# Moving transposed value blocks by GpSimd copies instead of transfers, in a two-layer decoder step on one core

## The reference

```python
for i in range(2):
    h = rms_norm(x, norm_pre[i])
    a, b, c, z = split(h @ w_in[i], 4)
    if i == 0:   o = b * conv3(c * a) * silu(z)
    else:        # a = q, b = forget gate, c = values; per head, f = lb + (1-lb)*sigmoid(b), k = 1-f
        # S_t = diag(f_t) S_{t-1} + k_t^T v_t ;  o_t = silu(q_t) S_t
        o = rms_norm(o_per_head, onorm) * silu(z)
    x = x + rms_norm(o @ w_out[i], norm_post[i])
```

## Time and profile before

| | us |
|---|---|
| median of 3 runs | 1010.6 (1010.59 to 1011.26) |
| the profiled execution, its own time | 1010.66 |
| its span in the trace | 1008.8 |
| TensorE busy | 1001.4 (99% of the span) |
| VectorE busy | 752.8 (75%) |
| ScalarE busy | 429.9 (43%) |
| GpSimd busy | 18.3 (2%) |

### The profile page before, as it was taken

How to read it: one execution, slowest core, us unless ns; L and a number is a source line. 1 busy time by engine, 2 the same in 40 slices (tenths; PEclk the granted TensorE clock), 3 DMA queues, 4 the chain that set the end, 5 groups by cost and what they waited for, 6 DMA issues and landing times.

```text
span 1008.8 us, 20437 instructions
## 1 busy us (share of the span) xinstructions
PE 1001.4 (99%) x7755; PEld 953.1 (94%) x7755; DVE 752.8 (75%) x1370; ACT 429.9 (43%) x879; POOL 18.3 (2%) x45
## 2 busy tenths in 40 slices
PE   9999999999999999999999999999999999999998
PEld 8999999999999987889999999999999999997886
DVE  6899677776776846873768979697897979686355
ACT  7444333333333524443344454444454454483222
POOL 2000000000000000000000000000000000000000
PEclk9999999999999999999999999999999999999999
DMA  8003122111211345843224033241424133162164
GB/s 259 23 22 84 43 63 63 42 42 45 80 42 42 123 140 180 265 167 89 59 64 128 23 102 88 65 109 57 127 62 105 44 95 95 62 192 94 36 229 181
DMA packets 139732, 96.62 MB, mean 96 GB/s; under 512 B 38822, under 2 KB 129399, under 8 KB 139687
## 3 DMA queue, kind: packets, MB, share of 16 engines
q1 hardware_dynamic: 117478, 80.74, 26.7%
q10 hardware_dynamic: 22208, 15.27, 5.0%
HBM read 71.53 MB, written 20.26 MB: 91 GB/s over the span
## 4 chain that ended last, share of the span: by engine, by line
PE 92%; DVE 5%; ACT 1%; issue 1%; DMA 0%; ACTq 0%; DVEq 0%
PE bank L741 34%; PE bank L798 28%; PE bank L886 13%; PE bank L766 4%; PE bank L1143 3%; PE bank L977 2%; PE bank L1092 1%; PE bank L1099 1%; PE bank L1101 1%; PE bank L868 1%; PE bank L1002 1%; PE bank L972 1%; DVE o_raw L1890 1%; PE bank L1034 0%; PE bank L1023 0%
## 5 line engine op out<-in xcount | busy, mean ns | idle before, releaser
L741 PE MATMUL bank<-reg_a,wsplit 128*128 128x352 f32 x2304 | 377.7, 324 | 0.5 <-ACT arena L1524 0.5
L741 PEld LDWEIGHTS bank<-reg_a,wsplit 128*128 128x128 f32 x2304 | 368.7, 188 | 1.9 <-issue 0.7
L798 PE MATMUL bank<-reg_a,wsplit 128*128 128x264 f32 x1344 | 165.6, 284 | 0.0
L798 PEld LDWEIGHTS bank<-reg_a,wsplit 128*128 128x128 f32 x1344 | 164.1, 188 | 0.1
L798 PE MATMUL bank<-reg_b,w_ring 128*128 128x264 f32 x1008 | 124.6, 284 | 0.0
L798 PEld LDWEIGHTS bank<-reg_b,w_ring 128*128 128x128 f32 x1008 | 123.3, 188 | 0.0
L886 PE MATMUL bank<-reg_b,reg_a 128*128 128x512 f32 x288 | 68.6, 396 | 0.0
L886 PEld LDWEIGHTS bank<-reg_b,reg_a 128*128 128x128 f32 x288 | 53.9, 188 | 13.0 <-issue 0.4
L2041 DVE TENSOR_TENSOR arena<-arena,bank 128x264 f32<-128x264 f32 x84 | 34.7, 426 | 34.1 <-PE bank L798 33.0
L1364 ACT ACTIVATE arena<-bank 128x264 f32<-128x264 f32 x84 | 32.2, 390 | 55.2 <-PE bank L798 50.5
L1342 ACT ACTIVATE w_ring<-wraw 128x512 fp32r<-128x512 f32 x42 | 26.1, 631 | 69.0 <-PE bank L798 69.0
(11 more groups left out here) (308 smaller groups left out, 1483.2 us busy)
## 6 DMA issues: line engine op xcount, KB each, us to landing
wraw<-in_w_in SPq DMA_DIRECT2D x64, 512.0 KB, 4.1
first_x<-in_x_prompt SPq DMA_DIRECT2D x8, 512.0 KB, 6.9
wraw<-in_w_out SPq DMA_DIRECT2D x8, 512.0 KB, 3.7
w_out_raw<-in_w_out SPq DMA_DIRECT2D x8, 512.0 KB, 5.0
arena<-in_w_out SPq DMA_DIRECT2D x8, 512.0 KB, 5.7
arena<-in_x_prompt SPq DMA_DIRECT2D x8, 512.0 KB, 4.2
x_scratch<-arena SPq DMA_DIRECT2D x8, 512.0 KB, 3.6
arena<-arena SPq DMA_DIRECT2D x128, 32.0 KB, 1.9
```

What stands on the lines that cost most here:

```text
L741: mm = nc.tensor.matmul(bank[b][:, 0:CH], w[wi][:, k, :], rhs[hi], start=(k == 0 and i == 0), stop=(k == KT - 1 and i == 2))
L798: mm = nc.tensor.matmul(bank[banks[q]][:, 0:QT], w[wi][:, k, :], B_OP[name][hi][:, k, q * QT:(q + 1) * QT], start=(start and k == 0 and i ...
```

## The change

There are three edits.

1. `move_values` goes from SyncE to GpSimd. It is called at the head of `set_places(h)`: it waits for `v_turned`, makes the same sixteen moves as `tensor_copy` instructions of 32 partitions by 256 values, adds one to `v_moved` after the last, and waits for that itself. SyncE's calls are gone.
2. The last head's keys are turned as those of the other heads: a transpose in blocks on VectorE, nine block copies there and seven on ScalarE. TensorE's eight transposes and ScalarE's two copies out of the banks are gone.
3. Before the loop, ScalarE's `evac("v", 1, ...)` stands between `turned_hi(6)` and `turned_hi(7)` and no longer behind both. On VectorE `turned(6)` comes before the reciprocal of row block 7 and no longer after that block's rows were scaled.

```diff
@@ sync
-            def move_values(h):
-                sp.wait_ge(v_turned, h + 1)
...
-                        sp.dma_start(rows[b * BLK:(b + 1) * BLK, d],
-                                     blocks[d * BLK:(d + 1) * BLK, b]).then_inc(v_moved, 16)
...
-                    if t == 2:
-                        move_values(j - 1)
...
-            move_values(KT - 1)
             sp.wait_ge(E_ACT.sem, E_ACT.at(0, "qc"))
...
-            sp.wait_ge(v_moved, KT * MOVED)
+            sp.wait_ge(v_moved, KT)
@@ gpsimd
+            def move_values(h):
+                pool.wait_ge(v_turned, h + 1)
...
+                for d in range(NQD):
+                    for b in range(NQD):
+                        ins = pool.tensor_copy(rows[b * BLK:(b + 1) * BLK, d], blocks[d * BLK:(d + 1) * BLK, b])
+                ins.then_inc(v_moved, 1)
+                pool.wait_ge(v_moved, h + 1)
+
             def set_places(h):
+                move_values(h)
                 pool.wait_ge(VR.sem, VR.at(h, "tt"))
@@ tensor
-                elif s == 8 and final:
-                    pe.wait_ge(VR.sem, VR.at(h, "w64"))
-                    for c in range(CK):
-                        mm = nc.tensor.transpose(bank[5 + c // 4][:, tokens(c % 4)], r_K[:, tokens(c)], ident[:, :])
-                    mm.then_inc(PR.now("kt"), 1)
                 elif s == 9:
                     pe.wait_ge(AR.sem, AR.at(h, "kt"))
-                    pe.wait_ge(v_moved, (h + 1) * MOVED)
-                    if not final:
-                        pe.wait_ge(k_moved, h + 1)
+                    pe.wait_ge(v_moved, h + 1)
+                    pe.wait_ge(k_moved, h + 1)
@@ scalar
             turned_hi(CK - 2)
+            evac("v", 1, G_IN2 + 2, None)
             turned_hi(CK - 1)
...
                 elif s == 8 and final:
-                    act.wait_ge(PR.sem, PR.at(h, "kt"))
-                    for half in range(2):
-                        ins = A(r_kt[:, half * 512:(half + 1) * 512], bank[5 + half][:, :], ACT.Copy)
-                    ins.then_inc(AR.now("kt"), 1)
+                    move_keys(h)
...
-                if n:
+                if n > 1:
                     evac("vqf"[i], c, G_IN2 + n + 1, None, VALUE_BANK if n == 4 else None)
@@ vector
                 if 2 <= i < BLOCK_ROWS:
                     turned(i - 2)
+                elif i == CK - 1:
+                    turned(i - 1)
                 dve.wait_ge(A_PO.sem, A_PO.at(i, "sd2"))
...
-            turned(CK - 2)
             turned_lo(CK - 2)
...
-                elif s == 8 and not final:
-                    dve.wait_ge(PR.sem, PR.at(h, "L32"))
+                elif s == 8:
+                    dve.wait_ge(PR.sem, PR.at(h, "L64" if final else "L32"))
```

More of the change, by code:

```diff
@@ L46 @@
 NQD = P // BLK
-MOVED = NQD * NQD * 16
 LANDED = NQD * 16
@@ L680, in _ @@
             pool.memset(r_as[:, :], 0.0).then_inc(pool_ev.now("as0"), 1)
+            def move_values(h):
+                pool.wait_ge(v_turned, h + 1)
+                blocks = r_vr[:, 0:NP].rearrange("p (c b t) -> p b c t", c=CK, b=NQD)
+                rows = r_vt[:, 0:NP].rearrange("p (d c v) -> p d c v", d=NQD, c=CK)
+                for d in range(NQD):
[3 more added lines that the diff above has]
+                pool.wait_ge(v_moved, h + 1)
             def set_places(h):
+                move_values(h)
                 pool.wait_ge(VR.sem, VR.at(h, "tt"))
@@ L1093, in rec @@
                                               start=True, stop=True)
-                    mm.then_inc(*(PR.many("u") if final else PR.many("kt", "u")))
+                    mm.then_inc(*PR.many("kt", "u"))
                 elif s == 10:
@@ L1520, in evac @@
                     if h is not None and c == 0:
-                        act.wait_ge(v_moved, (h + 1) * MOVED)
+                        act.wait_ge(v_moved, h + 1)
                         if lo is not None:
@@ L1566, in _, with move_keys @@
             turned_hi(CK - 2)
+            evac("v", 1, G_IN2 + 2, None)
             turned_hi(CK - 1)
+            def move_keys(h):
+                act.wait_ge(k_turned, h + 1)
+                for b, d in KEY_BLOCKS[0:KEYS_ACT]:
+                    out, blocks = key_block(b, d)
+                    ins = A(out, blocks, ACT.Copy)
+                ins.then_inc(AR.now("kt"), 1)
             def turn_hi(h, src=r_o):
@@ L2440, in gate_blocks @@
                 dve.wait_ge(o_landed, (h + 1) * LANDED)
-                dve.wait_ge(v_moved, (h + 2) * MOVED)
+                dve.wait_ge(v_moved, h + 2)
                 by_block = r_o[:, 0:NP].rearrange("p (b c t) -> p b c t", b=NQD, c=CK)
```

## The result

The changed kernel takes 1013.97 us (median of 7 runs, 1013.67 to 1014.27), the one before 1010.68 in the same runs: ratio 1.0031, 95% interval 1.0022 to 1.0040. The forecast was 1009.3, most likely no change that can be told; the kernel is slower by more than the 0.2% named there, and the time lies inside the range given. The profiled execution has a span of 1012.5 us.

A forecast was written before the change was run, and what follows sets the result against it. TensorE, busy 1001.4 of 1008.8 us, was taken to bound the kernel. Gains of 0.72 and 0.87 less 0.3 gave 1.3 us, hence 1009.3 against the median; range 1008.3 to 1021, the forecast case's own 1008.7 to 1010.4.

The forecast's parts named there:

- Edit 3: Before the loop, the second query group starts sooner, at 459.34 instead of 460.06: gain 0.72 us, bounds 0.48 and 0.72.
- Edit 2: In the last head, TensorE's eight key transposes come off the chain: gain 0.87 us, bounds 0.87 and 0.3.
- the copies' own cost: GpSimd's sixteen copies take 0.40 us each, 6.4 us for a head (3.8 to 11.1), hidden before the ones.
- a loss in the loop's heads below 0.81: In the loop's heads, VectorE's loss beside GpSimd's copies stays under the 0.81 us slack before `r_os`: zero on TensorE.
- The line that it read against the rival: GpSimd's zeroings over VectorE's work show no longer VectorE rows, though those read nothing; taken as evidence against rival A.
- 0.3 us for the last head: VectorE's slowing by the copies costs 0.3 us in the last head, where TensorE already waits for it.
- Rival A: Shared memory path: GpSimd copies and double-pace or two-input VectorE instructions take turns in each head; 1020.7 us, chance 0.30.
- Its lower case: Rival A at 0.24 us a copy: VectorE loses 1.1 us in a head, 1011.4 us.
- Rival B: VectorE always comes first, GpSimd starves, and its late ones hold `kq` about 1.1 us: 1010.8 us, chance 0.12.
- Rival C: The edits to the chain give more than counted, such as the last head's splits landing sooner: 1008.3 us, chance 0.08.

The follow-up runs named there:

- e10: The kernel before with edit 3 alone, the second values group evacuated sooner: 1010.11 us, ratio 0.9992 to before.
- e9: The kernel before with edit 2 alone, the last head's keys turned in blocks: 1009.76 us, ratio 0.9989 to before.
- e4: The changed kernel with eight of the sixteen blocks moved by GpSimd and the other eight by SyncE's transfers: 1009.02 us.
- e6: Against e1, GpSimd also makes 21 needless zeroings of 32x340, which only write: 1008.98 us.
- e7: Against e1, VectorE also makes one needless reciprocal (0.73 us) before the gates of each head: 1009.81 us.
- e11: The changed kernel with sixteen needless GpSimd copies more, after the moves and before the ones: 1052.25 us, ratio 1.0404 to before.
- e1: The changed kernel with the sixteen moves given back to SyncE's transfers, edits 2 and 3 staying: 1009.27 us, ratio 0.9984 to before.
- e8: Against e1, VectorE also makes two needless reciprocals (1.38 us) before the gates of each head: 1014.21 us.

## Why the prediction was wrong, point by point

**Edit 3** was right. The second query group follows the first without a gap. TensorE's timeline of after; the earlier trace rows had a wait of 0.48 at 460.06:

```profile
447.38 7.85 PE L739 MATMUL bank<-reg_a,wsplit 128*128 128x352 f32 x48
...
455.86 14.33 PE L739 MATMUL bank<-reg_a,wsplit 128*128 128x352 f32 x88
```

The 0.72 us forecast came; by e10, 0.8. VectorE is done with the moved `turned(6)` 0.41 us before ScalarE's root for row block 7 is there, so the move makes nobody late.

**Edit 2** was right. From the output projection's matmul at 919.89 to step 9 are 18.17 us, where there were 19.05 (915.24 to 934.29): 0.88 for 0.87 (e9 alone: 0.87). The keys of the last head, timelines of VectorE, ScalarE and TensorE after:

```profile
931.27 2.69 DVE L2563 COPY arena<-arena 32x256 f32<-32x256 f32 x9
...
933.94 2.97 ACT L1568 ACTIVATE arena<-arena 32x256 f32<-32x256 f32 x7
...
938.06 1.95 PE L1084 MATMUL bank<-arena 128*128 128x128 f32 x16
```

ScalarE ends at 936.9, the cover is 1.1 us, as worked out.

**Edit 1, the copies' own cost** was nearly right: 0.40 us for a copy was 0.396 as the median row and 0.43 from one to the next, "6.4 us for a head" was 6.9 alone, and even 9.8 beside VectorE is hidden before the ones are wanted.

**The step that failed** is "I take a loss in the loop's heads below 0.81 (zero on TensorE)". The loss is 1.37 to 1.41 us, and TensorE pays 0.72 in each of six heads. The bound of 0.81 was too wide as well: the slack is 0.65, since the weight load and not the matmul is the first to need `r_os`. Below it e4 and e6, with 0.50 and 0.42 us, cost nothing in the loop; at its edge e7, with 0.67, costs 0.03 for a head. No row stood behind the choice of a loss below 0.81: the prediction named the shared path, priced it at 1.1 to 5 us, and then forecast the one outcome below the whole of that estimate. The line that it read against the rival, that zeroings leave VectorE's rows as they are, says little of copies, as it says itself ("those read nothing"). Nor does it hold for all zeroings: in e6 they stretch VectorE's scalar instructions from 0.77 to 0.97. In the head read in before, the ones are written from 832.97 on, when the last double-pace instruction (L2419) has ended, so no row there could show it. Its 0.3 us for the last head was 0.7.

**Rival A** was the right mechanism on the right side, with the wrong size: 1020.7 against 1013.97. It took a whole copy, 0.40 us, for each contended VectorE instruction, some six of them. In the rows each loses 0.06 to 0.23 us, but over nine or so, since GpSimd is slowed as well and its copies take 9.8 us and not 6.4. Its lower case (VectorE loses 1.1 us, 1011.4) lies nearer. Worked with the measured loss and the prediction's slack the loop comes to 6 x (1.37 - 0.81) = 3.4, with the slack to the weight load to 6 x (1.37 - 0.65) = 4.3, and 4.3 came.

**Rival B**, that GpSimd starves and the ones hold `kq`, was not so here (ones at 840.25, `kq` at 844.55). It is what happens in e11, where `kq` is held for 3.7 us.

**Rival C**, more gain than counted, was not so: e1 has both gains and is at 1009.27, the sum's 1009.3.

The sum again with what was measured: 1010.7 - 0.72 - 0.88 + 4.3 + 0.7 = 1014.1, against 1013.97.

## What to carry to other kernels

Work put on GpSimd is not free because GpSimd is idle: beside it, VectorE loses a little at nearly every instruction that runs at double pace or reads two operands from SBUF (0.06 to 0.23 us here), and what counts is that loss against the slack of VectorE's next deadline. So work out the slack first, to the weight load where that is what waits, and where the rival's price lies above it, forecast the rival. If the move must be on GpSimd, start it where VectorE idles or reads from banks (after's two products with one input in a bank, L2593, take 1.29 us beside the copies, as they do in before), and keep it short; half of the blocks, or the same ones 3.0 us sooner, cost nothing.

## What the runs showed of the hardware

- A GpSimd copy of 32x256 takes 0.39 us, and 16 in a row 6.93 beside an idle VectorE, 9.83 beside a busy one (up to 1.30 for one; after).
- Copies (which read and write) stretch VectorE's one-input and scalar instructions of 128x1056 by 0.08 to 0.21 us and its two-input product of 128x1024 from 1.22 to 1.42 (after). Zeroings stretch the scalar ones (0.77 to 0.97) and no two-input one (e6).
- A needed operand was late for TensorE's weight load before it was late for the matmul: 0.65 us of slack where the matmul's start gave 0.81 (e7, e8, after).
- The two engines alternated, one instruction each, where the gates' instructions met the copies (e11). The Trainium skill, SBUF — State Buffer, section Who interferes with whom, says that the one that issued first holds the pair for its whole instruction and the other fully blocks. The alternation agrees; the price does not follow from it, since VectorE lost 0.14 us to a copy of 0.40.
- A stall of 4 us on TensorE was followed by a granted clock of 0.59 over the next 6.4 us (e11); after and e8, with stalls of 0.3 to 1.1 us, have a mean clock of 0.999 over the whole span.
